# Expert value sums of a two-layer decoder in four 64x64 quadrants of TensorE

## The chip, the cores and the metric

The kernel runs on one core of a Trainium2 chip, as one launch. The metric is its device time in microseconds; a time of the kernel before is the median of three runs. Profiles show one execution of the program.

## The reference

Two decoder layers on 256 tokens of width 1024, all in float32. Each layer has a mixer (gated linear and stick-breaking attention in layer 0, block attention and a linear recurrence in layer 1), a cross-attention into 256 memory tokens, and then an expert network, which is the part that matters here:

```python
def peer_ffn(xn, wq, subkeys, u, v):
    ...
        top_s, pos = lax.top_k(cand, K)                 # 8 heads, K = 16
        eidx = jnp.take_along_axis(cidx, pos, axis=-1)  # 128 experts of 16384 a token
        g = jax.nn.softmax(top_s, axis=-1)
        ue = u[eidx]
        ve = v[eidx]
        act = jax.nn.gelu(jnp.einsum('td,thkd->thk', xi, ue).astype(jnp.float32), approximate=False)
        return jnp.einsum('thk,thkd->td', (g * act).astype(ve.dtype), ve)
```

Every token picks 128 experts. For each it needs the expert's row of `u` (1024 numbers, for a dot product with the token) and its row of `v` (1024 numbers, which is added to the token's output with a weight).

## The kernel before

Activations are kept with features on the 128 partitions and tokens along the free axis; dense weights come through a ring of four 2 MB buffers, loaded from the SP queue. PSUM has eight banks of 512 float32 columns, given out in the order of a written list, `psum_jobs` (L153); `job(name)` in the TensorE program waits until the bank's last user has freed it, and `full`/`copied` (L411, L421) let the other engines wait for a bank's filling and emptying.

The expert network works in **units** (`UNITS = 256` a layer, 512 in all). Unit `u` is the `k`-th expert (of 128) of each of the 128 tokens of token tile `t`, `u = 128 t + k`. Its steps, each on an engine of its own:

- GpSimd (L1700 to L1712) gathers 128 rows of 8 KB, the `u` and the `v` row of each token's expert side by side, into one of eight slots of `arena`. Ahead of it stands `taken` (L455), the wait until the unit that used the slot eight units ago has been summed.
- VectorE (`unit`, L1416) multiplies the `u` half with the tokens and reduces: one number per token. While the first tile's units run, VectorE also does the routing (top-k) of the rest, in layer 0 and layer 1 alike.
- ScalarE (L1000 to L1007) applies the gelu, multiplies with the gate, and writes the 128 gains as a diagonal 128x128 matrix into one of four buffers (`diag`); ahead of the write it waits with `taken` for the unit four back.
- TensorE (L667 to L681) multiplies the diagonal with the slot's `v` half, 512 columns at a time, and adds up over the 128 units of a tile in two PSUM banks, `acc.0` and `acc.1`. The last matmul of a unit raises `expert_mm`, on which `taken` waits.

After 128 units ScalarE copies both banks to `yrow` (tokens on the partitions), TensorE turns `yrow` with eight 128x128 transposes into features on the partitions (`back`, L657), and VectorE adds the result to `xT` (L1423). For the first tile this happens a few units into the second tile; for the second tile it stands at the end of the layer, and in layer 1 at the end of the kernel, ahead of the store.

`mm` (L515) and so L516 is the line of nearly every matmul; a transpose in `back` is L663. L882 is the line of nearly all work on ScalarE. A float32 matmul leaves two records in the trace, each with a weight load of its own; a transpose leaves one.

Of the kernel before, what the change touches and what calls it, by code (L numbers as in the profile page):

```python
# [15 lines left out]
D = 1024  # L16
T = 256
M = 256
P = 128
# [4 lines left out]
BANK = 512  # L24
# [9 lines left out]
PE_H, PE_K, PE_KEYS, PE_DQ = 8, 16, 128, 128  # L34
EXPERTS = PE_KEYS * PE_KEYS
PAIRS = PE_H * PE_K
# [20 lines left out]
LEVELS = [P >> i for i in range(8)]  # L57
CONSTS = {}
for _name, _n in (("ident", P), ("ones", P), ("head_ones", P), ("rot", P), ("tri", P),
                  ("past", 3 * P), ("causal", 3 * P), ("iota", PE_K), ("inv_freq", 1),  # L60
                  ("levels", 8 * P)):
    CONSTS[_name] = (sum(n for _, n in CONSTS.values()), _n)
NCONST = sum(n for _, n in CONSTS.values())
# [3 lines left out]
UNITS = PAIRS * TT  # L67
DIAGS = 4
# [9 lines left out]
def constants():  # L78

    c = np.zeros((P, NCONST), np.float32)  # L80

    def put(name, a):
        at, n = CONSTS[name]
        c[:, at:at + n] = np.asarray(a, np.float32).reshape(P, n)

    p, f = np.arange(P)[:, None], np.arange(P)[None, :]
    put("ident", p == f)
    put("ones", np.ones((P, P)))
    put("head_ones", p // 64 == f // 64)

    rot = np.zeros((P, P))
    for m in range(P):
        half = m % 64 // 32
        rot[m + 32 if half == 0 else m - 32, m] = -1.0 if half == 0 else 1.0
    put("rot", rot)
    put("tri", p >= f)

    put("past", np.concatenate([p < f, np.ones((P, P)), p < f], 1))

    low = np.where(f <= p, 0.0, -1e30)  # L100
    put("causal", np.concatenate([low, np.zeros((P, P)), low], 1))

    lev = [(p // (2 * m) == f // (2 * m)) & (p % (2 * m) < m) & (f % (2 * m) >= m) for m in LEVELS[1:]]
    put("levels", np.concatenate(lev + [p == f], 1))
    put("iota", np.broadcast_to(np.arange(PE_K), (P, PE_K)))
    put("inv_freq", 10000.0 ** (-(np.arange(P) % 32).astype(np.float64) * 2 / MO_D))
    return c
# [105 lines left out]
def trunk(nc, d, out_d):  # L213
# [8 lines left out]
    with ExitStack() as ctx:  # L222
# [3 lines left out]
        def sem(name):  # L226
            return ctx.enter_context(nc.semaphore(name))
# [27 lines left out]
        iota = sb("iota_bf", [P, PE_K], BF)  # L255
        ones_row = cst[:, CONSTS["ones"][0]:CONSTS["ones"][0] + 1].to_broadcast([P, T])

        def const(name):
            at, n = CONSTS[name]
            return cst[:, at:at + n]  # L260
# [5 lines left out]
        ident, ones, head_ones = const("ident"), const("ones"), const("head_ones")  # L266
# [78 lines left out]
        yrow = kv[:, 0:D]  # L345
        dots = red[:, PAIRS:2 * PAIRS]

        diag = const('levels').rearrange('p (n m) -> p n m', m=P)[:, 0:DIAGS, :]
# [54 lines left out]
        gelu_done = sem("gelu_done")  # L403
        gain_done = sem("gain_done")
        weighed = sem("weighed")
        expert_mm = sem("expert_mm")
        stored = sem("stored")

        block = ctx.enter_context(nc.Block())
# [44 lines left out]

        def taken(eng, l, u):  # L455

            eng.wait_ge(expert_mm, l * UNITS + u + 1)


        @block.sync  # L460
# [36 lines left out]
        def _(pe):  # L497
            seen = [0]

            def job(name):  # L500

                n = JOB[name]
                assert n == seen[0], (name, n, seen[0])
                seen[0] += 1
                if n >= BANKS:
                    pe.wait_ge(psum_free[n % BANKS], n // BANKS)
                return psum[:, n % BANKS, :], psum_full[n % BANKS]
# [7 lines left out]
            def mm(out, lhsT, rhs, start=True, stop=True):  # L515
                return nc.tensor.matmul(out, lhsT, rhs, start=start, stop=stop)  # L516
# [117 lines left out]
            def peer(l):  # L634
                b = AT[f"sub{l}"]
                sub = ring[:, b % RING, 0:16 * PE_KEYS].rearrange("p (c n) -> p c n", n=PE_KEYS)
                for g in range(4):
                    w = weights(f"pq{l}{g}")
                    for i in range(2):
                        features(f"pq{l}.{2 * g + i}", w, 2 * P * i, hT, norm=f"ffn{l}" if g == i == 0 else None)  # L640
                    for n in X_ROWS[g]:
                        o, done = job(f"xr{l}.{n}")
                        for c in range(4):
                            last = nc.tensor.transpose(o[:, c * P:(c + 1) * P],
                                                       hT[:, 4 * (n % 2) + c, (n // 2) * P:(n // 2 + 1) * P], ident)
                        last.then_inc(done, 1)
                    copied(pe, f"pq{l}.{2 * g}", f"pq{l}.{2 * g + 1}")
                    if g == 0:
                        pe.wait_ge(w_loaded[b % RING], 16 * (b // RING + 1))
                    for t in range(TT):  # L650
                        o, done = job(f"ps{l}.{4 * t + g}")
                        for c in range(4):
                            last = mm(o[:, c * P:(c + 1) * P], qpT[:, g % 2, c, t * P:(t + 1) * P],
                                      sub[:, 4 * g + c, :])
                        last.then_inc(done, 1)

                def back(t):  # L657

                    copied(pe, f"acc{l}.{t}.0", f"acc{l}.{t}.1")
                    for b in range(2):  # L660
                        o, done = job(f"back{l}.{t}.{b}")
                        for c in range(4):
                            last = nc.tensor.transpose(o[:, c * P:(c + 1) * P],  # L663
                                                       yrow[:, (4 * b + c) * P:(4 * b + c + 1) * P], ident)
                        last.then_inc(done, 1)

                for t in range(TT):  # L667
                    (o0, done0), (o1, done1) = job(f"acc{l}.{t}.0"), job(f"acc{l}.{t}.1")
                    for k in range(PAIRS):
                        u = t * PAIRS + k  # L670
                        pe.wait_ge(weighed, l * UNITS + u + 1)
                        v = slot[slot_of(u)][:, D:2 * D]
                        first = mm(o0, diag[:, u % DIAGS, :], v[:, 0:BANK], k == 0, k == PAIRS - 1)
                        last = mm(o1, diag[:, u % DIAGS, :], v[:, BANK:D], k == 0, k == PAIRS - 1)
                        if k == PAIRS - 1:
                            first.then_inc(done0, 1)
                        last.then_inc(expert_mm, 1)
                        if u == PAIRS + BACK_LAG + 1:
                            back(0)
                    pe.wait_ge(expert_mm, l * UNITS + (t + 1) * PAIRS)  # L680
                    pe.sem_inc(done1, 1)  # L681
                back(1)


# [6 lines left out]
            o, done = job("gg")  # L691
            for k in range(KC):
                last = mm(o[0:GLA_RANK, 0:T], w_gg[:, k, :], hT[:, k, :], k == 0, k == KC - 1)
            last.then_inc(done, 1)
            copied(pe, "gg")
            o, done = job("gate")
            for a in range(2):
                last = mm(o[:, a * T:(a + 1) * T], gate_up[:, a * P:(a + 1) * P], ggT[0:GLA_RANK, :])
# [15 lines left out]
            for li in range(len(LEVELS) + 1):  # L714
# [7 lines left out]
                for par in range(2):  # L722
                    r = slice(64 * par, 64 * par + 64)
# [15 lines left out]
            for i in range(2):  # L739
                o, done = job(f"glao{i}")  # L740
# [1040 lines left out]
```

## Time and profile before

| | |
|---|---|
| median of 3 runs | 1932.71 us (1931.68 to 1933.12) |
| span of the profiled execution | 1928.8 us |
| TensorE matmul busy | 1591.4 us (83%), 4638 records |
| VectorE, ScalarE, GpSimd busy | 52%, 34%, 27% |
| mean granted TensorE clock | 0.984 of 2.4 GHz |
| bytes moved by DMA | 610.20 MB, of which the gathers 536.90 MB |

The span is from the first instruction to the last; the runs' time has some microseconds around it. A matmul's busy time in the records includes the time until its result is out, so records in a row overlap. Layer 0's gather begins near 302 us and its stream ends near 990, layer 1's runs from 1247 to near 1920.

### The profile page before, as it was taken

The numbers are of one execution on the slowest core, as the hardware profiler recorded it, in microseconds if no ns is written. First come the engines' busy times: TensorE is split into PE (matmuls) and PEld (weight loads), VectorE is DVE, ScalarE is ACT, GpSimd is POOL, SyncE is SP. The second block draws the span as 40 slices with busy tenths as digits, with TensorE's granted clock in tenths as the row PEclk, the third lists the DMA queues.
The fourth block names the chain that finished last, engine by engine and source line by source line (L and its number), as shares of the span: only waits on it lengthen the run. The fifth ranks groups of instructions, "written<-read, shape, count | busy, mean of one in ns | idle before, by whom it ended". The sixth has DMA issues, their size and how long they took to land.

```text
span 1928.8 us, 15560 instructions
## 1 busy us (share of the span) xinstructions
PE 1591.4 (83%) x4638; PEld 806.3 (42%) x4638; DVE 1011.3 (52%) x2487; ACT 646.9 (34%) x1897; POOL 514.9 (27%) x516
## 2 busy tenths in 40 slices
PE   7999989767877877787779989997788777877876
PEld 4777778222322222222237666763232222222222
DVE  3432238688544554445441632489874445444454
ACT  1243221423433333333332433123343333333333
POOL 0000001434433433333300000015444343333331
PEclk9999999999999999999989999999999999999999
DMA  8321224999999999999933222359999999999996
GB/s 304 131 88 44 101 108 184 390 416 421 422 421 422 421 422 422 421 421 422 421 154 131 88 104 93 118 221 422 421 421 421 422 421 421 422 421 422 421 421 287
DMA packets 107540, 610.20 MB, mean 316 GB/s; under 512 B 10032, under 2 KB 10176, under 8 KB 41280
## 3 DMA queue, kind: packets, MB, share of 16 engines
q0 software_dynamic: 73728, 536.90, 67.1%
q1 hardware_dynamic: 33728, 72.30, 10.3%
q8 instruction: 37, 0.61, 0.1%
q14 instruction: 47, 0.39, 0.1%
HBM read 608.12 MB, written 1.05 MB: 316 GB/s over the span
## 4 chain that ended last, share of the span: by engine, by line
DMA 45%; PE 38%; DVE 9%; ACT 5%; issue 2%; POOL 0%; SPq 0%; DVEq 0%; PEldq 0%; ACTq 0%
DMA arena<-in_experts,idxT 45%; PE psum L516 37%; DVE arena L1416 5%; ACT cst L882 1%; ACT gains L882 1%; ACT arena L882 1%; ACT gelus L882 1%; ACT L882 1%; DVE red L1385 1%; DVE kv L1377 0%; POOL arena L1710 0%; DMA vecs<-in_vecs 0%; ACT sqb L882 0%; DVE kv L1383 0%; DVE red L1200 0%
## 5 line engine op out<-in xcount | busy, mean ns | idle before, releaser
L516 PE MATMUL psum<-arena,cst 128*128 128x512 f32 (+2 forms) x2112 | 1029.4, 616 | 283.6 <-ACT cst L882 279.1
L1416 DVE CUSTOM_DVE_ANT_0 arena<-arena,xrow 128x1024 f32<-128x1024 f32 x512 | 624.4, 1224 | 537.7 <-DMA arena<-in_experts,idxT 537.0
L1710 POOL DMA_INDIRECT arena<-in_experts,idxT x512 | 514.7, 1005 | 1387.8 <-PE psum L516 790.0
L516 PEld LDWEIGHTS psum<-arena,cst 128*128 128x128 f32 x2112 | 367.1, 191 | 942.5 <-ACT cst L882 645.7
L882 ACT ACTIVATE gelus<-red 128x1 f32<-128x1 f32 x512 | 103.6, 202 | 770.2 <-DVE red L1416 769.9
L516 PE MATMUL psum<-hT,ring 128*128 128x256 f32 x1280 | 293.3, 390 | 6.1 <-DVE hT L1215 6.1
L516 PEld LDWEIGHTS psum<-hT,ring 128*128 128x128 f32 x1280 | 248.9, 196 | 47.5 <-issue 9.8
L882 ACT ACTIVATE cst<-cst,gains 128x128 f32<-128x128 f32 x512 | 206.2, 403 | 23.2 <-PE psum L516 6.7
L882 ACT ACTIVATE gains<-gelus,gateT 128x1 f32<-128x1 f32 x512 | 150.8, 294 | 17.0 <-ACT gelus L882 0.2
L882 ACT ACTIVATE arena<-psum 128x512 f32<-128x512 f32 (+3 forms) x89 | 47.8, 545 | 304.3 <-PE psum L516 304.0
L516 PE MATMUL psum<-mixT,ring 128*128 128x256 f32 x256 | 57.4, 387 | 2.5 <-DVE mixT L1689 2.5
L516 PE MATMUL psum<-arena 64*128 64x128 f32 (+4 forms) x320 | 52.0, 317 | 4.9 <-DVE arena L1521 2.4
L516 PEld LDWEIGHTS psum<-mixT,ring 128*128 128x128 f32 x256 | 49.7, 195 | 10.8 <-DVE mixT L1689 3.3
L1223 DVE TENSOR_TENSOR xT<-xT,psum 128x512 f32<-128x512 f32 x16 | 11.0, 688 | 72.8 <-PE psum L516 72.8
L516 PE MATMUL psum<-ring,arena 128*128 128x128 f32 (+1 forms) x192 | 44.6, 384 | 2.9 <-issue 2.9
L516 PEld LDWEIGHTS psum<-arena 64*128 64x128 f32 (+2 forms) x320 | 35.7, 177 | 20.0 <-issue 10.5
L1416 DVE DVE_READ_ACCUMULATOR2_ANT red<- 128x1 f32 x512 | 42.5, 83 | 0.0
L516 PE MATMUL psum<-ring,hT 128*128 128x512 f32 x96 | 42.3, 595 | 0.0
L882 ACT ACTIVATE sqb<-xT 128x512 f32<-128x512 f32 x24 | 14.4, 625 | 81.2 <-DVE xT L1223 77.3
L516 PEld LDWEIGHTS psum<-ring,arena 128*128 128x128 f32 x192 | 27.1, 191 | 18.3 <-issue 17.8
L1533 DVE COPY_PREDICATED arena<-cst,psum 128x512 f32<-128x512 int32 x16 | 11.7, 730 | 40.7 <-PE psum L516 40.4
L516 PE MATMUL psum<-arena,ring 128*128 128x256 f32 x128 | 28.1, 380 | 1.6 <-ACT arena L882 1.6
(161 smaller groups left out, 672.1 us busy)
## 6 DMA issues: line engine op xcount, KB each, us to landing
ring<-in_peer_wq SPq DMA_DIRECT2D x8, 2048.0 KB, 8.1
ring<-in_ev_w_in SPq DMA_DIRECT2D x6, 2048.0 KB, 11.8
ring<-in_od_w_in SPq DMA_DIRECT2D x5, 2048.0 KB, 33.0
ring<-in_xa_wkv SPq DMA_DIRECT2D x4, 2048.0 KB, 7.9
arena<-in_experts,idxT POOLq DMA_INDIRECT x512, 15.3
ring<-in_ev_w_out SPq DMA_DIRECT2D x2, 2048.0 KB, 7.8
ring<-in_xa_wq SPq DMA_DIRECT2D x2, 2048.0 KB, 9.2
ring<-in_xa_wo SPq DMA_DIRECT2D x2, 2048.0 KB, 7.7
```

The source lines that it names most:

```text
L516: return nc.tensor.matmul(out, lhsT, rhs, start=start, stop=stop)
L882: return nc.scalar.activation(out, in_, f, **k)
L1223: V.tensor_tensor(x2, x2, pairs(o), ALU.add).then_inc(bank_free(name), 1)
L1385: link(V.tensor_reduce(eidx[:, cols], h_.rearrange("p (n c) j -> p n (c j)", c=2), X, ALU.add))
L1416: V.tensor_tensor_reduce(out=ut, in0=ut, in1=xrow[:, u // PAIRS, :], scale=1.0, scalar=0.0, op0=ALU.mult, op1=ALU.add, accum_out=dots[:, k ...
L1533: ins = V.copy_predicated(attn[:, par].rearrange("p a t q -> p (a t) q"), msk, o.rearrange("p (n q) -> p n q", q=P))
L1710: nc.gpsimd.indirect_dma_start(slot[slot_of(u)], None, d["experts"], bass.IndirectOffsetOnAxis(ap=idxT[:, u:u + 1], axis=0))\
```

## The change

Each unit's value sum was two matmuls with a 128x128 diagonal, one for each half of the 1024 columns. Now it is four, each with a 64x64 diagonal block: rows 0 to 63 and 64 to 127 of the slot separately (the other two blocks of a diagonal matrix are zero). For the first 512 columns the rows go straight: rows 0 to 63 of the slot to partitions 0 to 63 of the bank. For the last 512 columns they go crossed: rows 0 to 63 to partitions 64 to 127. So the four matmuls use the four 64x64 quadrants of the array. `expert_mm` becomes two semaphores, one for each half of the rows, and `taken` waits for both. Both banks of a tile are signalled as done after the last unit has ended on both halves; before, the first bank was signalled by its own last matmul. The crossed bank is put straight in `back`: its four blocks are multiplied with a permutation matrix, `swap`, which is new among the constants, and the other four with the identity; both are float32 matmuls and no longer transposes.

```diff
-                  ("past", 3 * P), ("causal", 3 * P), ("iota", PE_K), ("inv_freq", 1),
+                  ("past", 3 * P), ("causal", 3 * P), ("iota", PE_K), ("inv_freq", 1), ("swap", P),
...
+    put("swap", (p + 64) % P == f)
...
-        expert_mm = sem("expert_mm")
+        expert_mm = [sem(f"expert_mm{r}") for r in range(2)]
...
         def taken(eng, l, u):
 
-            eng.wait_ge(expert_mm, l * UNITS + u + 1)
+            for r in range(2):
+                eng.wait_ge(expert_mm[r], l * UNITS + u + 1)
...
                         for c in range(4):
-                            last = nc.tensor.transpose(o[:, c * P:(c + 1) * P],
-                                                       yrow[:, (4 * b + c) * P:(4 * b + c + 1) * P], ident)
+                            last = mm(o[:, c * P:(c + 1) * P], yrow[:, (4 * b + c) * P:(4 * b + c + 1) * P],
+                                      const("swap") if b else ident)
                         last.then_inc(done, 1)
...
-                    (o0, done0), (o1, done1) = job(f"acc{l}.{t}.0"), job(f"acc{l}.{t}.1")
+                    acc = [job(f"acc{l}.{t}.{b}") for b in range(2)]
                     for k in range(PAIRS):
                         u = t * PAIRS + k
                         pe.wait_ge(weighed, l * UNITS + u + 1)
                         v = slot[slot_of(u)][:, D:2 * D]
-                        first = mm(o0, diag[:, u % DIAGS, :], v[:, 0:BANK], k == 0, k == PAIRS - 1)
-                        last = mm(o1, diag[:, u % DIAGS, :], v[:, BANK:D], k == 0, k == PAIRS - 1)
-                        if k == PAIRS - 1:
-                            first.then_inc(done0, 1)
-                        last.then_inc(expert_mm, 1)
+                        for b in range(2):
+                            for r in range(2):
+                                rows_in = slice(64 * r, 64 * r + 64)
+                                col = 64 * (r ^ b)
+                                o, done = acc[b]
+                                last = mm(o[col:col + 64], diag[rows_in, u % DIAGS, rows_in],
+                                          v[rows_in, b * BANK:(b + 1) * BANK], k == 0, k == PAIRS - 1)
+                                if b == 1:
+                                    last.then_inc(expert_mm[r], 1)
                         if u == PAIRS + BACK_LAG + 1:
                             back(0)
-                    pe.wait_ge(expert_mm, l * UNITS + (t + 1) * PAIRS)
-                    pe.sem_inc(done1, 1)
+                    for r in range(2):
+                        pe.wait_ge(expert_mm[r], l * UNITS + (t + 1) * PAIRS)
+                    for o, done in acc:
+                        pe.sem_inc(done, 1)
                 back(1)
```

## Rows read from the trace of the kernel before

**Rows 1.** The page: its head and the engines' busy time, share and instructions.
```profile
span 1928.8 us, 15560 instructions
PE 1591.4 (83%) x4638; PEld 806.3 (42%) x4638; DVE 1011.3 (52%) x2487; ACT 646.9 (34%) x1897; POOL 514.9 (27%) x516
```
**Rows 2.** The page's chain that ended last, shares of the span by engine.
```profile
DMA 45%; PE 38%; DVE 9%; ACT 5%; issue 2%; POOL 0%; SPq 0%; DVEq 0%; PEldq 0%; ACTq 0%
```
**Rows 3.** Stretches: busy us and count by engine, clock, DMA share, GB/s.
```profile
600.00:700.00 100.00, 80.34 (x171) 28.18 (x170) 50.94 (x83) 36.97 (x122) 38.60 (x41) 1.00 1.01 422
360.00:370.00 10.00, 6.87 (x15) 2.12 (x13) 6.28 (x22) 2.70 (x9) 3.30 (x4) 1.00 1.02 414
400.00:430.00 30.00, 18.55 (x37) 6.58 (x37) 24.98 (x103) 9.00 (x30) 10.63 (x9) 0.97 1.02 417
970.00:980.00 10.00, 7.93 (x16) 2.71 (x16) 4.94 (x8) 3.63 (x13) 1.73 (x2) 1.00 1.02 424
```
**Rows 4.** Timeline, 601 to 605 us: start, duration, instruction [idle before, releaser].
```profile
601.81 1.98 PE L516 MATMUL psum<-arena,cst 128*128 128x512 f32 x4 [0.50 <-ACT cst L882]
...
604.30 1.98 PE L516 MATMUL psum<-arena,cst 128*128 128x512 f32 x4 [0.50 <-ACT cst L882]
```
**Rows 5.** The gathers' line L1710: from issue to landing.
```profile
DMA to landing us min/median/max: 5.3/15.3/22.7
```
**Rows 6.** Timeline of TensorE: 64-row matmuls in two halves, and 128-row ones.
```profile
51.82 0.72 PE L516 MATMUL psum<-arena 64*128 64x128 f32 x8 [2.36 <-DVE arena L1521]
...
61.26 1.71 PE L516 MATMUL psum<-arena 64*128 64x128 f32 x16
...
125.67 3.81 PE L516 MATMUL psum<-arena 128*128 128x128 f32 x32 [1.15 <-DVEq L1548]
```
**Rows 7.** Chain at the start, and the issue of the first constants load.
```profile
1.66 6.21 DMA vecs<-in_vecs
...
cst<-in_consts SPq DMA_DIRECT2D x1, 712.5 KB, 6.2
```
**Rows 8.** The page's DMA queues that carry instructions: packets, MB, share.
```profile
q8 instruction: 37, 0.61, 0.1%
q14 instruction: 47, 0.39, 0.1%
```
**Rows 9.** Start of layer 1's stream: timeline of GpSimd and TensorE, then stretches.
```profile
1284.19 1.43 POOL L1710 DMA_INDIRECT arena<-in_experts,idxT  x1 [28.14 <-PE psum L516]
1289.92 0.93 POOL L1710 DMA_INDIRECT arena<-in_experts,idxT  x1 [4.30 <-PE psum L516]
1292.73 0.94 POOL L1710 DMA_INDIRECT arena<-in_experts,idxT  x1 [1.88 <-PE psum L516]
...
1287.09 22.54 PE L516 MATMUL psum<-arena,cst 128*128 128x512 f32 x48 [3.17 <-ACT cst L882]
...
1290.00:1292.00 2.00, 2.00 (x4) 0.79 (x3) 1.93 (x7) 0.75 (x3) 0.85 (x1) 0.57 0.29 57
1292.00:1294.00 2.00, 2.00 (x6) 0.82 (x5) 1.97 (x15) 0.79 (x3) 0.94 (x1) 1.00 0.90 356
```
**Rows 10.** Timeline of the tail of layer 0, from the last unit's matmuls.
```profile
989.90 1.98 PE L516 MATMUL psum<-arena,cst 128*128 128x512 f32 x4 [0.50 <-ACT cst L882]
...
991.12 0.60 ACT L882 ACTIVATE kv<-psum 128x512 f32<-128x512 f32 x1 [1.27 <-PE psum L516]
992.01 0.60 ACT L882 ACTIVATE kv<-psum 128x512 f32<-128x512 f32 x1 [0.29 <-PEq L681]
...
992.71 1.06 PE L663 MATMUL psum<-cst,kv 128*128 128x128 f32 x8 [0.82 <-ACT kv L882]
993.37 1.29 DVE L1423 TENSOR_TENSOR xT<-xT,psum 128x512 f32<-128x512 f32 x2 [4.55 <-PE psum L663]
```
**Rows 11.** Timeline: the same pair of matmul records at either level of the clock.
```profile
998.98 1.22 PE L516 MATMUL psum<-red,cst 128*128 128x256 f32 x2 [5.21 <-DVE red L1200]
...
87.40 0.59 PE L516 MATMUL psum<-red,cst 128*128 128x256 f32 x2
```

## The prediction

> **What bounds the kernel now.** I read the page's shares first, then the chain that ended last, then the stretches, then single units. TensorE is the busiest engine by time, 83% [rows 1], and that is the trap of this profile: the chain that ended last runs through DMA for 45% and through TensorE for 38% [rows 2]. The stretches say which of the two it is in the gather. From 600 to 700 us TensorE is busy 80.34 us of 100 while the DMA engines stand at a share of 1.01 and move 422 GB/s [rows 3]; near the stream's end it is 424 GB/s. One unit is one gather of 128 rows of 8 KB, 1.049 MB, so 422 GB/s is one unit each 2.485 us. The timeline shows just that pace: TensorE starts a unit at 601.81 and the next at 604.30, and its four matmul records take 1.98 us, after which it idles 0.50 [rows 4]. A gather lands 15.3 us (median) after its issue [rows 5], which is six units of 2.485 us: the requests wait in a queue. A slot that comes free earlier only makes that queue longer. So a faster value sum is worth nothing in the steady stream, and is worth something only where DMA is not full or the stream has ended: the first units of layer 1, and the tail behind each layer's last unit. The other side of it: TensorE costs nothing more as long as a unit keeps it under 2.485 us.
>
> **What a unit costs after the change.** Before: 2 matmuls of 512 columns, 4 records (an fp32 matmul leaves two), (1.98 - 0.26) / 4 = 0.43 us each and 0.26 for the last to drain [rows 4]. (The same 0.26 is left over in the 32 records of 128 columns that take 3.81 us: 0.11 each [rows 6].) After: 4 matmuls of 64 x 64, 8 records, of 0.43 us each since the 512 columns stay. What counts is how many run side by side. The trace of before has 64-row matmuls, the upper half of the rows and then the lower: 8 of them took 0.72 us, where 8 in line would take 8 x 0.11 + 0.26 = 1.14; 16 took 1.71, in line 2.02 [rows 6]. So two row halves do overlap, well when few are queued on each. Nothing in the trace runs two column halves of the same rows side by side. Bounds for a unit, in recorded time: all four together 2 x 0.43 + 0.26 = 1.12 us; row halves together and column halves staggered by one record 3 x 0.43 + 0.26 = 1.55; column halves in line 4 x 0.43 + 0.26 = 1.98 (as now); nothing together 8 x 0.43 + 0.26 = 3.70. I take 1.55, since the rows show overlap of different parts of the array with fp32 and since two records of one quadrant must follow each other.
>
> **The sum, part by part**, against the profiled span of 1928.8 us; the median of the runs is 1932.71, 3.9 us more, and I add that at the end.
> - *Constant table.* `swap` adds 128 columns, 64 KB, to the first constants load. The first chain item is the DMA of `vecs` just behind it, 6.21 us, on a 712.5 KB load of 6.2 us [rows 7]: 64/712.5 of the 6.2 us would be 0.5, if that load alone set the time; at 422 GB/s it is 0.16. I take +0.2.
> - *Steady stream.* 0, covered by the DMA queue [rows 3, 4, 5]. The second `wait_ge` in `taken` stands before each diagonal on ScalarE and before each gather on GpSimd. GpSimd's issue takes 0.94 us of 2.485 [rows 9] and its wait is for the slot anyway; behind it on its queue are only later gathers. ScalarE's wait is for a unit four back. Both row halves of a unit end together within a record. 0.
> - *More instructions.* 8 more records a unit (4 matmul, 4 weight load) are 4096. The two instruction queues moved 0.61 + 0.39 MB for 15560 instructions [rows 1, 8], 64 bytes each, so 0.26 MB more, on engines that are full: +0.6 us. If they are fetched elsewhere it is 0.
> - *First units of layer 1.* There DMA is starved: GpSimd issues at 1284.19, then only at 1289.92 and 1292.73, released by TensorE's 48 records that begin at 1287.09; DMA moves 57 GB/s from 1290 to 1292 and 356 in the next 2 us, with the clock at 0.57 in the first of these [rows 9]. With units of 1.55 us (twice as long while the clock is low) I put the second and third issue at about 1288.7 and 1290.3, 1.2 and 2.4 us earlier; every later unit of the layer moves with DMA. Bounds: 0 (units as slow as now) to -3.5 (units of 1.12, and the slow filling up to full rate shortened as well). I take -2.4. In layer 0 this doesn't pay, since weight loads fill DMA there: at 360 to 370 us it moves 414 GB/s at 1.02 with TensorE busy 6.87 of 10 [rows 3].
> - *Tail of each layer, twice.* Now: last unit starts at 989.90; the copy of the first half begins at 991.12, as soon as the first matmul is done, the second at 992.01; transposes 992.71, 8 records in 1.06 us; the two additions from 993.37, 1.29 us for both [rows 10]. After: both signals come only after the whole unit. With 1.55 us the copies begin near 991.6 and 992.2, +0.2 for the second. The transposes become fp32 matmuls, 16 records x 0.11 + 0.26 = 2.02 us instead of 1.06; the second addition can't begin before they end, so the pair ends 0.8 us later. Together +1.0 a layer at full clock. At the lower clock a pair of 256-column records takes 1.22 us instead of 0.59 [rows 11]; then the unit ends about 1.6 us later than now and the 16 records cost some 2.7 more, +4.3. Which clock? In the ramps TensorE is busy 6.87 of 10 us and holds 1.00, and from 400 to 430 it is busy 18.55 of 30 and is granted 0.97 [rows 3]; 1.55 of 2.485 is 62%, the same share. I take +1.8 a layer, nearer the full clock: +3.6.
>
> Sum: 0.2 + 0.6 - 2.4 + 3.6 = +2.0. Span 1930.8, time **1934.7 us**. The transposes of the first token tile lie inside the stream and are covered by the 15.3 us queue.
>
> **The rule against this change.** The trace shows 64-row halves overlapping, but each half wrote a bank of its own there [rows 6]. The Trainium skill, "PSUM — Partial Sum Buffer", section "PSUM bank collisions raise a hardware error", says that different row tiles must not access one PSUM bank at the same time. In this change both row halves write one bank, in different partition halves. By that rule, kept by waiting, the time would be that of rival 3. No run here shows it.
>
> **Rivals.**
> 1. *Column halves in line*: the change doesn't do what it says beyond the row halves. Units stay 1.98 us. For it: no row shows column halves together. No gain in layer 1; the tail pays 0.6 for the later first signal and 0.8 for the matmuls: 0.8 + 0 + 2.8 = +3.6, 1936.3.
> 2. *The clock stays at the lower level through the streams.* TensorE streams for less of each unit than now, and the lower level came after stretches in which it did little: 0.57 from 1290 to 1292, after idling 3.17 us before 1287.09 [rows 9]. Units (pitch at most 1.72 us, one unit overlapping the next) still fit under 2.485, but both tails run low: 0.8 - 1.5 + 8.6 = +7.9, 1940.6.
> 3. *One bank at a time.* Both row halves write the same bank, which no row shows, and wait for each other there. Of the four matmuls only the second and third (other rows, other bank) overlap, and the fourth with the next unit's first: three steps of 0.86 and 0.26, 2.84 us for a unit, but a pitch of 1.72, so DMA still sets the stream. Tail: second copy 1.5 later, matmuls 0.8: 0.8 + 4.6 = +5.4, 1938.1.
> 4. *TensorE becomes the bound, clearly slower.* From a pitch of 2.485 us on, each 0.1 us costs 51 us over 512 units. Nothing overlapping is 3.44 us of streaming: 512 x 0.95 = +490, about 2420. The same happens with rival 1 at the lower clock. Against it: the overlapping row halves.
> 5. *All four together at full clock*: 0.8 - 3.5 + 2 x 0.55 = -1.6, 1931.1, no measurable change.
> 6. *Faster*: the longer queue moves DMA from 422 to the 424 GB/s of one stretch [rows 3]: 0.5% of 1272 us is -6, 1928. Against it: share 1.01 already.
>
> **How the numbers follow.** Forecast 0.40 (own range 1932 to 1938), rivals in order 0.20, 0.16, 0.06, 0.07, 0.07, 0.04. About 0.2%, 3.9 us, is what a measurement here tells from no change, so "same" is 1928.8 to 1936.6. Same: 0.36 of the forecast, 0.14 of rival 1, 0.03 of 2, 0.02 of 3, all 0.07 of 5, 0.62. Slower: 0.04 + 0.06 + 0.13 + 0.04 + 0.07 = 0.34. Faster 0.04. The range 1930.5 to 1941.5 leaves out rivals 4 and 6 and the ends of the others.
>
> **What would show each step.** In the stretches of the gather: 422 GB/s and share 1.01 unchanged, units still 2.485 us apart, median landing time longer by what the unit became shorter. A unit's 8 records in about 1.55 us; 1.98 is rival 1, 2.84 rival 3. Granted clock in the stream: near 1 or well below tells the forecast from rival 2. In layer 1 the second gather issued before 1289.9 less whatever the start moved. In the tail, 16 records instead of 8 ahead of the additions and both copies behind one signal. The prediction is wrong if a unit's pitch passes 2.485 us, or if DMA's rate in the stream moves at all.

## The result, and the profile after

The kernel after takes 1933.62 us (median of 20 runs, 1931.27 to 1937.56); the kernel before, run beside it, 1931.01 (20 runs, 1928.13 to 1933.89). The ratio is 1.0014, 95% interval 1.0008 to 1.0021: slower by 2.7 us, with 1.5 to 4.1 in the interval, and within the 0.2% that the prediction calls no change. The prediction's time was 1934.7 us. Ratios and intervals here are estimates from all the runs of a pair and not quotients of the two medians, which scatter more. The profiled executions have spans of 1928.8 us before and 1932.9 us after.

The page after: head, engines, clock in 40 slices, chain, one instruction queue, the gathers' line.

```profile
span 1932.9 us, 20212 instructions
PE 1454.1 (75%) x6718; PEld 604.0 (31%) x6718; DVE 1011.8 (52%) x2487; ACT 646.7 (33%) x1897; POOL 703.2 (36%) x516
...
PEclk9999999656666676666669999997766667666666
...
q8 instruction: 53, 0.87, 0.2%
...
DMA 39%; PE 35%; DVE 9%; issue 7%; POOL 7%; ACT 4%; POOLq 0%; SPq 0%; ACTq 0%; DVEq 0%; PEldq 0%
...
L1718 POOL DMA_INDIRECT arena<-in_experts,idxT x512 | 703.0, 1373 | 1203.4 <-DVE idxT L1394 579.2
```

TensorE's busy time fell by 137 us against [rows 1], and none of it reached the end. Three things are new. The clock row reads 5 to 7 throughout both gather streams, where the mean before was 0.984. GpSimd is busy 188 us more with the same 516 instructions: one gather's issue takes 1373 ns on average (0.94 us at best, 1.9 for many). And the chain has 7% GpSimd and 7% issue where [rows 2] has none and 2%.

The stretches after: busy us and count of PE, PEld, DVE, ACT, POOL, then clock, DMA share, GB/s.

```profile
500.00:600.00 100.00, 69.67 (x320) 10.87 (x312) 49.92 (x83) 38.88 (x123) 60.49 (x40) 0.64 1.01 421
600.00:700.00 100.00, 70.27 (x340) 13.89 (x344) 50.74 (x83) 36.96 (x122) 60.60 (x41) 0.67 1.01 421
```

The last two numbers are those of [rows 3] within 1 GB/s, the clock is not. The timeline of TensorE after, from 602 us: start, duration, instruction, idle time before.

```profile
602.53 1.99 PE L518 MATMUL psum<-arena,cst 64*64 64x512 f32 x8 [0.51 <-ACT cst L890]
605.02 1.78 PE L518 MATMUL psum<-arena,cst 64*64 64x512 f32 x8 [0.50 <-ACT cst L890]
607.50 1.09 PE L518 MATMUL psum<-arena,cst 64*64 64x512 f32 x8 [0.70 <-ACT cst L890]
```

The starts are 2.48 to 2.49 us apart, as in [rows 4]. A unit's eight records take 1.09 us at the upper level of the clock (2.4 GHz) and 1.99 at the lower (1.2 GHz), which is about what [rows 4] shows for the old unit at the upper level (1.98). All four quadrants do run together, and the stream swings between the two levels.

### Where the time went in the trace

The trace can be cut at events that both kernels have. In the table a stream runs, for layer 0, from the first gather's issue to the start of the last unit's dot product on VectorE, and for layer 1 from the start of the first dot product to that of the last; a tail runs from there to the start of the next layer's norm matmul, or to the end; the middle is from that matmul to layer 1's first gather, code that no kernel here touches, with the time that it spent at the lower clock beside it. All are us of the profiled executions. Two stretches are left out: the start up to the first gather, which takes from 300.95 to 303.11 us in these executions and differs by 0.9 between the two of the kernel before, and the 24.0 us from layer 1's first gather to its first dot product. *Null* and *again* are second copies of before and after, the other names are the experiments below.

| kernel | stream 0 | tail 0 | middle (low clock) | stream 1 | tail 1 | span |
|---|---|---|---|---|---|---|
| before | 685.5 | 11.39 | 248.7 (16.3) | 645.7 | 11.41 | 1928.8 |
| null | 685.4 | 11.39 | 248.5 (16.0) | 644.8 | 11.42 | 1926.6 |
| after | 685.6 | 12.65 | 251.6 (25.4) | 643.2 | 13.31 | 1932.9 |
| again | 685.5 | 12.67 | 251.6 (25.4) | 643.2 | 13.30 | 1932.9 |
| straight | 685.5 | 11.89 | 248.5 (16.0) | 646.3 | 11.90 | 1930.8 |
| back_mm | 685.7 | 12.19 | 251.3 (25.1) | 645.9 | 12.21 | 1932.2 |
| freeswap | 685.1 | 11.86 | 248.7 (16.3) | 644.5 | 12.74 | 1929.3 |
| warm | 685.1 | 11.88 | 251.3 (25.1) | 644.6 | 11.86 | 1930.1 |
| warm_free | 685.2 | 11.86 | 252.3 (30.1) | 644.8 | 11.13 | 1932.4 |
| extra256 | 685.3 | 11.38 | 252.3 (30.1) | 645.5 | 11.40 | 1931.7 |
| extra512 | 696.9 | 18.77 | 251.0 (24.8) | 662.5 | 19.16 | 1974.4 |

Before to after: tails +1.3 and +1.9, stream 1 -2.5 (-1.6 against null), stream 0 nothing, the middle +2.9. The middle is longer where it spent more time at the lower clock, and the edit is not in it.

The timeline of both tails after, from the last unit's matmuls to the second addition: layer 0,

```profile
990.57 1.85 PE L518 MATMUL psum<-arena,cst 64*64 64x512 f32 x8 [0.52 <-ACT cst L890]
...
992.63 1.08 ACT L890 ACTIVATE kv<-psum 128x512 f32<-128x512 f32 x2 [2.12 <-PEq L689]
...
993.82 2.02 PE L518 MATMUL psum<-cst,kv 128*128 128x128 f32 x16 [1.40 <-ACT kv L890]
...
995.88 0.69 DVE L1431 TENSOR_TENSOR xT<-xT,psum 128x512 f32<-128x512 f32 x1 [0.20 <-PE psum L518]
```

and layer 1.

```profile
1921.91 1.09 PE L518 MATMUL psum<-arena,cst 64*64 64x512 f32 x8 [0.83 <-ACT cst L890]
...
1923.20 1.08 ACT L890 ACTIVATE kv<-psum 128x512 f32<-128x512 f32 x2 [1.34 <-PEq L689]
...
1924.38 3.47 PE L518 MATMUL psum<-cst,kv 128*128 128x128 f32 x16 [1.39 <-ACT kv L890]
...
1927.89 0.69 DVE L1431 TENSOR_TENSOR xT<-xT,psum 128x512 f32<-128x512 f32 x1 [0.73 <-PE psum L518]
```

In layer 0 the last unit ran at the lower level (1.85 us) and the turning matmuls at the upper (2.02, the value worked out from [rows 6]); from the unit's start to the end of the additions are 6.00 us, where [rows 10] has 4.76. In layer 1 it is the other way round: a unit of 1.09 us lets turning begin 2.47 us after the unit's start, earlier than the 2.81 of [rows 10], and then the 16 records take 3.47 us. The price of the tail depends on the piece on which the low clock falls.

The start of layer 1's stream after, on GpSimd, and the stretches behind it.

```profile
1288.97 1.42 POOL L1718 DMA_INDIRECT arena<-in_experts,idxT  x1 [28.15 <-PE psum L518]
1294.06 0.94 POOL L1718 DMA_INDIRECT arena<-in_experts,idxT  x1 [3.67 <-PE psum L518]
1295.77 1.08 POOL L1718 DMA_INDIRECT arena<-in_experts,idxT  x1 [0.77 <-PE psum L518]
```

```profile
1294.00:1296.00 2.00, 2.00 (x16) 0.77 (x12) 1.19 (x3) 1.87 (x8) 1.17 (x2) 0.51 0.46 102
1296.00:1298.00 2.00, 2.00 (x24) 0.85 (x20) 1.90 (x14) 1.57 (x6) 1.66 (x2) 1.00 0.80 315
```

After the first issue the second comes 5.09 us later and the third 6.80; in [rows 9] it was 5.73 and 8.54. So 0.6 and 1.7 us are won there, at a low clock (0.51) as before.

### What GpSimd's longer issues are

GpSimd's issues are not longer because slots come free earlier. Four lines of GpSimd's timelines, the first two of after, then one of warm (an experiment below: units of 1.09 us throughout) and one of straight (units of 1.93 us):

```profile
602.85 1.92 POOL L1718 DMA_INDIRECT arena<-in_experts,idxT  x1 [0.57 <-issue]
609.42 0.94 POOL L1718 DMA_INDIRECT arena<-in_experts,idxT  x1 [0.85 <-PE psum L518]
```

```profile
602.99 0.94 POOL L1724 DMA_INDIRECT arena<-in_experts,idxT  x1 [1.55 <-PE psum L518]
```

```profile
602.85 1.97 POOL L1718 DMA_INDIRECT arena<-in_experts,idxT  x1 [0.50 <-issue]
```

I read the traces unit by unit, for units 100 to 249 of layer 0. In after, where the unit that freed the slot ran at the lower level of the clock (1.9 us and more, 92 units) the issue took 1.90 us in the median; where it ran at the upper level (under 1.15 us, 32 units) it took 0.94. So the long issues go with the slots that come free late. What makes an issue long is not shown, and nothing in the stream waits for it: its pace is that of before.

The same reading shows what the second wait in `taken` costs. From the end of the unit eight back to the issue that it releases are 0.27 us in before, null, back_mm and extra256, with one semaphore, and 0.81 to 0.83 in straight, after, again, freeswap, warm and warm_free, with two. No run has the second semaphore by itself, so this may in part be the row halves. The time from a gather's issue to its dot product is 15.34 us before, 15.67 in warm and 14.93 in after: with units 0.89 us shorter throughout, 0.56 goes into the later issue and 0.33 into a longer wait for DMA.

### The profile page after: what moved, and what is told of

It reads as the page before. It is cut to its first block, busy times and chain, and to the rows that moved or that the text cites. A ratio compares the mean times of both kernels' runs of the same rounds, so it can differ in the third digit from the quotient of the medians.

```text
span 1932.9 us, 20212 instructions
## 1 busy us (share of the span) xinstructions
PE 1454.1 (75%) x6718; PEld 604.0 (31%) x6718; DVE 1011.8 (52%) x2487; ACT 646.7 (33%) x1897; POOL 703.2 (36%) x516
## 4 chain that ended last, share of the span: by engine, by line
DMA 39%; PE 35%; DVE 9%; issue 7%; POOL 7%; ACT 4%; POOLq 0%; SPq 0%; ACTq 0%; DVEq 0%; PEldq 0%
DMA arena<-in_experts,idxT 38%; PE psum L518 34%; POOL arena L1718 7%; DVE arena L1424 5%; ACT cst L890 1%; ACT gains L890 1%; ACT arena L890 1%; ACT gelus L890 1%; DVE red L1393 0%; DVE kv L1385 0%; DMA vecs<-in_vecs 0%; ACT sqb L890 0%; DVE rstd L1316 0%; DVE rstd L1304 0%; DVE red L1208 0%
## 5 line engine op out<-in xcount | busy, mean ns | idle before, releaser
L518 PE MATMUL psum<-arena,cst 64*64 64x512 f32 (+1 forms) x4160 | 881.0, 928 | 424.7 <-ACT cst L890 417.6
L1718 POOL DMA_INDIRECT arena<-in_experts,idxT x512 | 703.0, 1373 | 1203.4 <-DVE idxT L1394 579.2
L518 PEld LDWEIGHTS psum<-arena,cst 64*64 64x64 f32 (+1 forms) x4160 | 155.5, 178 | 1144.0 <-ACT cst L890 1099.2
```

Source lines behind the costliest of these rows:

```text
L1718: nc.gpsimd.indirect_dma_start(slot[slot_of(u)], None, d["experts"], bass.IndirectOffsetOnAxis(ap=idxT[:, u:u + 1], axis=0))\
```

## Experiments

Medians are in us; each ratio is against the kernel before, run beside it in one of three groups: warm, freeswap, warm_free and back_mm (median of before there 1930.37, 33 runs), straight, extra256, extra512 and thin_before (1929.55, 23), the others (1931.09, 23).

### How many quadrants run together, and what the crossing brings

*straight* takes the kernel after and sends both column halves of a row half through the same quadrant, so nothing is crossed and `back` keeps its transposes.

```diff
-                                col = 64 * (r ^ b)
+                                col = 64 * r
...
-                            last = mm(o[:, c * P:(c + 1) * P], ..., const("swap") if b else ident)
+                            last = nc.tensor.transpose(o[:, c * P:(c + 1) * P], ..., ident)
```

> The changed kernel with both halves of the columns straight: rows 0 to 63 to partitions 0 to 63 in both banks, so two of the four quadrants are used; turning by transposes. Tells what the crossing does. If quadrants are what runs side by side, a unit takes 1.98 us at full clock instead of 1.09, row halves together and column halves in line. The clock then tells what it follows: near 1 if it follows the time that TensorE is at work, near 0.65 or below if it follows how much of the array is at work; at the lower clock with half the array a unit streams for 3.44 us, over 2.485, and the time goes up by hundreds of us. Otherwise time 1932 to 1934.

Measured: 1933.83 (11 runs), ratio 1.0018 (1.0009 to 1.0026). Timeline of one unit and the stretch from 600 us of straight:

```profile
602.59 1.93 PE L518 MATMUL psum<-arena,cst 64*64 64x512 f32 x8 [0.56 <-ACT cst L890]
```

```profile
600.00:700.00 100.00, 78.72 (x330) 20.09 (x332) 50.75 (x83) 37.01 (x123) 74.49 (x41) 1.00 1.01 421
```

The row halves run together (nothing together would be 3.70 us), the column halves in line. It is the crossing that takes a unit from 1.93 to 1.09 us, and it is also what takes the clock from 1.00 to 0.67: with TensorE busy 78.72 of 100 us the level held, with 70.27 it did not. In both kernels the two row halves write one bank, in different partitions, and neither waited for the other: with waits there a unit of after would be 2.84 us (rival 3) and one of straight 3.70. The Trainium skill, "PSUM — Partial Sum Buffer", "PSUM bank collisions raise a hardware error", quotes both wordings: row tiles not in one bank at a time, and two engines free to use one bank as long as their accesses lie in different quadrants of it. The runs behave as the second, which is said there of two engines. The Trainium skill, "TensorE: Matmul & The Clock Gate", section "Measured speedup vs the span model", says that a pack of tiles takes the time of one matmul plus some nanoseconds a tile; 1.09 us for four against 2 x 0.43 + 0.26 = 1.12 agrees.

### Is the low clock the price?

*warm* adds to the kernel after, ahead of each unit's wait, four matmuls with a block of zeros as weights, in the same four quadrants, so that TensorE is busy more of each unit (all units but the first and the last of a tile).

```diff
+                        for b in range(2 if 0 < k < PAIRS - 1 else 0):
+                            for r in range(2):
+                                rows_in = slice(64 * r, 64 * r + 64)
+                                col = 64 * (r ^ b)
+                                mm(acc[b][0][col:col + 64], const("causal")[rows_in, P:P + 64],
+                                   cst[rows_in, 0:BANK], False, False)
                         pe.wait_ge(weighed, l * UNITS + u + 1)
```

> The changed kernel, and ahead of each unit's wait for its diagonal four more 64x64 matmuls with zeros as weights (they add zero), for all units but the first and last of a tile. They fill TensorE's idle time. Theory (the lower granted clock costs in the tails): the clock in the stream rises from 0.65 to near 1, the last unit and the 16 records of the turning run at full clock, each layer's tail 0.5 to 1.5 us shorter; 1 to 2.5 us less than the changed kernel's 1933.6, so 1931 to 1932.5, ratio to the kernel before 1.000. Rival (the loss is in the extra instructions and the constant): no gain, or 0.6 us more for 4000 more records, 1934.

Measured: 1934.01 (11), ratio 1.0019 (1.0010 to 1.0028). Timeline and stretch of warm:

```profile
601.97 1.04 PE L518 MATMUL psum<-cst 64*64 64x512 f32 x8
603.55 1.09 PE L518 MATMUL psum<-arena,cst 64*64 64x512 f32 x8 [0.54 <-ACT cst L896]
```

```profile
600.00:700.00 100.00, 79.93 (x644) 22.94 (x640) 50.45 (x83) 36.98 (x122) 40.17 (x40) 0.97 1.01 421
```

The clock came back to 0.97 with TensorE busy 79.93, and the tails fell from 1.26 and 1.90 above before to 0.49 and 0.45. So the low clock costs 0.8 and 1.4 us in the tails. The stream did not move by it at all. The median did not follow the tails: 1931 to 1932.5 was expected, and it is 1934.0, no better than after's. "What the clock does outside the streams" has what is known of that.

### What the crossed bank costs at the end

*back_mm* takes the kernel before and only turns with matmuls instead of transposes.

```diff
-                            last = nc.tensor.transpose(o[:, c * P:(c + 1) * P], ..., ident)
+                            last = mm(o[:, c * P:(c + 1) * P], ..., ident)
```

> The kernel before with the turning steps alone changed: float32 matmuls with the identity instead of transposes. By the prediction's step (16 records instead of 8, the pair of additions ends 0.8 us later) +0.8 us in each layer's tail, +1.6 in all, ratio 1.0008. Rival: the additions hide it, 0.

Measured: 1934.44 (11), ratio 1.0019 (1.0010 to 1.0028). Timeline of its tail of layer 0:

```profile
991.73 2.02 PE L516 MATMUL psum<-cst,kv 128*128 128x128 f32 x16 [0.83 <-ACT kv L882]
992.89 0.69 DVE L1423 TENSOR_TENSOR xT<-xT,psum 128x512 f32<-128x512 f32 x1 [5.05 <-PE psum L516]
993.79 0.69 DVE L1423 TENSOR_TENSOR xT<-xT,psum 128x512 f32<-128x512 f32 x1 [0.20 <-PE psum L516]
```

Each tail is 0.80 us longer, the step's own number; the time is up by more, 3.7 us by the ratio, and the rest is not in the tails. With straight (+0.50, +0.49, the later first signal alone) the two parts add up to 1.30; the tail of layer 0 after has 1.26.

*freeswap* takes the kernel after, keeps the transposes, and lets VectorE put the crossed bank straight, by two additions of half the tokens each.

```diff
+                        o = o.rearrange("p (c n) -> p c n", n=P)
+                        if b:
+                            step(V.tensor_tensor(xs[:, :, 0:64], xs[:, :, 0:64], o[:, :, 64:P], ALU.add))
+                            xs, o = xs[:, :, 64:P], o[:, :, 0:64]
+                        V.tensor_tensor(xs, xs, o, ALU.add).then_inc(bank_free(f"back{l}.{t}.{b}"), 1)
```

> The changed kernel with the eight turning steps as transposes again; the crossed bank is put straight by the addition on VectorE, which reads the token halves of the transposed bank in swapped order (two additions of half the width). Theory (the float32 matmuls of the turning cost 1 us at full clock and 1.7 to 2 at the lower one in each tail): 8 records instead of 16, 1 to 1.5 us shorter per tail, together 2 to 3 us less than the changed kernel, 1931. Rival (that time is hidden behind the additions): under 0.5 us, 1933.4.

Measured: 1931.15 (11), ratio 1.0003 (0.9994 to 1.0012). Timeline of its tail of layer 0:

```profile
992.27 1.94 PE L665 MATMUL psum<-cst,kv 128*128 128x128 f32 x8 [1.39 <-ACT kv L890]
...
994.25 0.42 DVE L1433 TENSOR_TENSOR xT<-xT,psum 128x256 f32<-128x256 f32 x1 [0.17 <-PE psum L665]
994.59 0.41 DVE L1435 TENSOR_TENSOR xT<-xT,psum 128x256 f32<-128x256 f32 x1
```

Even with the eight transposes at the lower clock (1.94 us, against 1.06 in [rows 10]) this tail is 0.8 us shorter than after's, and that of layer 1 0.6, where 1 to 1.5 each was expected. Of the versions with four quadrants this one and the next, warm_free, have intervals that take in no change; both keep the transposes.

*warm_free* is both edits in one.

> Both of the edits above together: zero matmuls between the units and transposes with the swap in the addition. If tails are where the change loses and the start of layer 1 where it gains about 1 to 2.5 us, this one is faster than the kernel before by 1 to 3 us: 1928 to 1930, ratio 0.9985 to 0.9995. If the gain at the start of layer 1 is not real, it is equal to the kernel before.

Measured: 1929.95 (11), ratio 0.9993 (0.9984 to 1.0002). The last tail, all of it at the upper clock, is 0.28 us shorter than before's; the tail of layer 0 is 0.47 longer. It is the best version of the four quadrants that was tried, and its gain can't be told from zero.

### Who sets the pace of the stream

*extra256* and *extra512* take the kernel before and add to each unit one matmul with weights of zero, of 256 or 512 columns.

```diff
+                        if 0 < k < PAIRS - 1:
+                            mm(o1[:, 0:256], const("causal")[:, P:2 * P], v[:, BANK:BANK + 256], False, False)
                         last = mm(o1, diag[:, u % DIAGS, :], v[:, BANK:D], k == 0, k == PAIRS - 1)
```

> The kernel before with one more matmul of 256 columns with zero weights in each unit. A unit's streaming goes from 1.72 to 2.15 us, still under the 2.485 us in which DMA delivers a unit. Theory (DMA sets the stream): the stream unchanged; +0.4 us at the start of layer 1, and 4000 fewer... no more than +1.5 us in all, ratio under 1.001. Rival (TensorE's time counts in the chain for 38%): +0.43 us x 512 = +220 us.

Measured: 1932.97 (12), ratio 1.0010 (1.0001 to 1.0018); both streams as before (table).

> The kernel before with one more matmul of 512 columns with zero weights in each unit: streaming 6 x 0.43 = 2.58 us, over 2.485. Theory (TensorE is free up to DMA's pace and sets the stream from there): +0.1 us x 508 units = +48 us, and up to 20 more for what a unit waits between its neighbours; TensorE busy near 100% in the stream, DMA share under 1. Rival (a unit must also wait for its diagonal, so gaps stay): +0.5 us or more x 508, +250.

Measured: 1976.23 (5), ratio 1.0238 (1.0224 to 1.0251). The stretch from 500 us of extra512:

```profile
500.00:600.00 100.00, 100.00 (x234) 44.27 (x233) 49.01 (x82) 37.99 (x120) 41.44 (x39) 1.00 1.00 407
```

TensorE work of 0.43 us more a unit lengthens neither stream, 0.86 more costs about 46 us: the edge lies between a pitch of 2.15 and one of 2.58 us, and the 2.485 us of a gather are in that interval. A unit of 1.98 + 0.86 = 2.84 in recorded time has a pitch of 6 x 0.43 = 2.58, 0.095 over it, or 49 us in 512. In the table the streams hold 28 us of it and the tails 15, since TensorE is by then behind VectorE.

### The gain where DMA does not bind

*half_before* and *half_after* gather rows of 4 KB instead of 8 after the first eight units (each slot's second half keeps what the first gather put there), with the same edit in both kernels.

```diff
+                    w_ = 2 * D if u < SLOTS else D
+                    table = d["experts"] if u < SLOTS else d["experts"].rearrange("e (h n) -> (e h) n", n=D)
-                    nc.gpsimd.indirect_dma_start(slot[slot_of(u)], None, d["experts"],
+                    nc.gpsimd.indirect_dma_start(slot[slot_of(u)][:, 0:w_], None, table,
```

> The kernel before, but from the ninth unit of a layer on each gather brings 4 KB rows instead of 8 KB, into the slot's first half alone; the values that are summed are what lay in the slot's second half, so the output is not the reference's, and the work of all engines but DMA is the same. DMA then needs 1.24 us a unit. Theory (TensorE hides behind DMA, by 0.76 us a unit): TensorE becomes the bound, about 1.72 to 1.8 us a unit, near 100% busy; the first 60 units of a layer are paced by VectorE's routing and stay, some 400 of 512 units shrink by 0.7 us: about 1640. Rival (something else paces units at 2.485): 1932.

Measured: 1596.72 (4), ratio 0.8267 (0.8253 to 0.8281).

> The same cut of the gathers in the changed kernel. Theory (four quadrants halve TensorE's share of a unit and the gain is only covered by DMA in the real kernel): a unit is then paced by VectorE (1.31 us) or DMA (1.24), not by TensorE (0.86 at full clock); against the same cut without the change 400 x 0.4 us = 160 less, about 1480. If the clock falls and stays at its lower level, a unit takes 1.72 us of TensorE again and both kernels are equal. This tells whether the clock eats the gain where TensorE would be the bound.

Measured: 1544.84 (4), ratio 0.8006 (0.7994 to 0.8018). The stretch from 600 us, half_before and then half_after:

```profile
600.00:700.00 100.00, 100.00 (x240) 44.72 (x239) 71.17 (x117) 52.74 (x176) 71.79 (x58) 1.00 0.87 298
```

```profile
600.00:700.00 100.00, 70.28 (x516) 13.76 (x506) 78.92 (x129) 56.83 (x191) 73.54 (x64) 0.98 0.93 335
```

Here TensorE is the bound before the change (busy 100 of 100, 58 units in 100 us by GpSimd's count) and stops being it: 64 units, clock 0.98. The same edit now gives 51.9 us, 3.2%. What limits it then is not shown; DMA's share rose from 0.87 to 0.93 and VectorE's busy time from 71 to 79, so DMA is the nearer to full. I had expected 1640 and 1480. The pace before was the 1.72 us a unit that I had named (58 in 100 us), but 335 us less are some 440 units at 0.76 us each, where I took 400 at 0.7; the pace after was 1.56 us, where I had named 1.31.

*thin_before* was a first try at the same: every other gather on the kernel before fetches 16 rows instead of 128.

```diff
+                    n = 16 if (u + u // SLOTS) % 2 else P
+                    nc.gpsimd.indirect_dma_start(slot[slot_of(u)][0:n], None, d["experts"],
+                                                 bass.IndirectOffsetOnAxis(ap=idxT[0:n, u:u + 1], axis=0))\
```

> The kernel before with every other gather cut to 16 of its 128 rows (the other rows keep what lay there: the values of those rows are wrong, the work of all engines but DMA is the same). DMA needs 1.4 us a unit instead of 2.485. Theory: TensorE becomes the bound, 1.72 us a unit at 83% or more busy; the streams of 600 + 600 us shrink by 0.76 x about 480 units, time near 1570.

Measured: 1736.89 (4), ratio 0.8978 (0.8947 to 0.9009), against 1570 expected. The stretch from 600 us:

```profile
600.00:700.00 100.00, 85.83 (x194) 35.59 (x194) 56.96 (x96) 43.33 (x145) 55.28 (x48) 0.98 0.96 282
```

DMA is still at a share of 0.96, moving 282 GB/s. At 48 units in 100 us that is 2.0 us of DMA a unit instead of 2.5, with 56% of the bytes: by this estimate a gather of 16 rows takes some 1.5 us of DMA time against 2.5 for 128. No engine is full, so the run doesn't say what a bound by TensorE would give; the half pair does.

### What the clock does outside the streams

*null* is the kernel before and *again* the kernel after, both unchanged.

> The kernel before once more, unchanged. Every theory expects a ratio of 1; it tells how far medians of some ten runs lie apart by themselves, and whether the stretch of lower clock near 1090 to 1097 us, which some profiles have and the first one had not, comes and goes without any edit.

Measured: 1929.67 (12 runs) against 1931.09 (23), ratio 1.0000 (0.9991 to 1.0008). Two medians of one kernel differ by 1.4 us.

> The changed kernel once more, unchanged, beside the unchanged kernel before. Expected 2 to 3 us over it, as first measured, with 1 to 2 us of it in the two tails, the start of layer 1 giving 1 us back, and the rest coming or going with the place at which the clock falls near 1000 and 1090 us.

Measured: 1933.06 (11), ratio 1.0013 (1.0004 to 1.0021). Span and all segments repeat those of after within 0.2 us.

The middle has about 248.6, 251.3 or 252.3 us and 16, 25 or 30 us of low clock. It is the same within 0.2 us in both copies of before and in both of after, and differs between programs whose code is equal there. One stretch where they part, before and then after:

```profile
1090.00:1100.00 10.00, 8.70 (x42) 5.97 (x43) 7.15 (x19) 6.89 (x19) 0.00 (x0) 1.00 0.00 0
```

```profile
1090.00:1100.00 10.00, 8.65 (x35) 5.86 (x34) 6.87 (x22) 5.40 (x15) 0.00 (x0) 0.83 0.00 0
```

The same shows over the runs, since each has its mean clock. Among the 33 runs of before in the first group those with a mean clock of 0.981 to 0.983 have spans of 1930 to 1932 us in the mean for each clock value, those of 0.984 to 0.987 of 1928 to 1929: 0.6 us for each 0.001 of clock (correlation -0.67; 0.7 and 0.8 in the two other groups). warm_free's profiled execution (1932.4, clock 0.977) is its slowest; its median span is 1928.1. So a comparison of two profiled executions of this kernel carries up to some 4 us of clock luck in dense code.

The slope holds within a kernel and doesn't carry from one to another. Warm and warm_free have the same median clock, 0.979 against before's 0.984, and 0.6 us for 0.001 would make both 3.0 us slower; warm is 3.6 slower and warm_free 0.4 faster. Nor does it fit back_mm: median clock 0.982, and no such slope within its 11 runs. By their ratios warm and back_mm are 3.7 us over before, straight 3.5 and extra256 1.9, while their tails and streams explain about 0, 1.6, 1.8 and 0. So some 2 us, and more in warm, are not located in four edited kernels, and null, with nothing edited, has a median 1.4 us lower than before's. Why the middle falls into one of three lengths, and whether an edit far from it picks one, stays open; with the clock of after's streams in the mean, its runs can't be split this way.

## Why the prediction was right or wrong

The verdict, a change within 0.2%, came from the right mechanism: DMA covers the value sum. That the time itself was met, 1934.7 against 1933.62, is in part luck. The forecast stood on a median before of 1932.71 (three runs) where twenty gave 1931.01, so its +2.0 is to be held against +2.7, and the parts of that +2.0 came out less well than their sum.

- **DMA sets the stream: right.** Stream 0 is 685.1 to 685.7 us in each kernel up to the edge of 2.485 us, at 421 or 422 GB/s and a share of 1.01, whether a unit takes 1.09, 1.93, 1.98 us or, as in extra256, more. Extra512 and the half pair show the bound from both sides. The sign that I named for the cover, a landing time longer by what the unit became shorter, was not seen in that size: in warm, with units 0.89 us shorter, a gather waits 0.33 us longer, and in after 0.41 us less.
- **The second wait in `taken`, 0: wrong in size, harmless in the stream.** Kernels with it issue a gather 0.55 us later after the slot came free. The stream covers that. The start of layer 1 does not: in straight, with units as long as before, the third issue comes 9.03 us after the first (1285.12 to 1294.15) where [rows 9], null and back_mm have 8.54.
- **A unit of 1.55 us: wrong.** It is 1.09, rival 5's 1.12. [rows 6] has small matmuls in two row halves that overlap in part, and I carried "in part" over to 512 columns. The number that mattered was the one record's streaming time plus the drain.
- **The clock stays near full: wrong in the streams, half right where it counts.** I argued that TensorE kept 0.97 at 62% busy and 1.00 at 69% in the ramps; at 70% the stream had 0.67. The premise of rival 2 came true. But the level swings, and the tails met it for one piece each: +1.26 and +1.90 against my 1.8 each and rival 2's 4.3. The sum of the two, 3.2 against 3.6, was close because a unit that was too long stood in for a clock that was too high. Its parts by themselves held: 0.8 for the matmuls (back_mm 0.80), 0.5 for the later signal (straight; I had 0.6).
- **The start of layer 1, -2.4: the right sign, the size in doubt.** Stream 1 is 643.2 in both executions against a mean of 645.5 in before, null and back_mm, -2.2. But null alone is 0.9 below before, and the other three with four quadrants have 644.5 to 644.8, about -0.8. The second and third issues came 0.6 and 1.7 us earlier relative to the first, where I had 1.2 and 2.4; the second wait's 0.55 is about what is missing. Straight, with units of 1.93, gains nothing, as rival 1 had it.
- **Constants, +0.2: in line with the traces.** The first TensorE matmul starts at 11.37 to 11.69 us in the seven executions with `swap` (mean 11.57) and at 11.24 to 11.47 in the seven without (mean 11.32). The ranges overlap, so the size is as forecast only in the mean.
- **More instructions, +0.6: no sign.** The queue q8 grew from 0.61 to 0.87 MB, the 0.26 worked out, and in warm to 1.38, and stream 0 was not longer in either (685.6, 685.1).
- **Missed: the middle.** I gave unchanged code no term, and it holds 2.9 of the 4.1 us between the two profiled executions. Tails, stream 1 and constants sum to 3.2 - 2.2 + 0.2 = +1.2; the other 1.5 of the medians' +2.7 could be half of the middle's, and no run settles it.

## What to carry to other kernels

Ask what binds in the stretch, not which engine is busiest: here the same edit halved TensorE's time for a unit and gave 3.2% where TensorE was full and nothing where DMA was. Work taken from a covered engine is not free either, if the engine then does so little that its clock falls and the next dense piece starts at the lower level. Below some 4 us, cut the trace at shared events and run the kernel before twice, since code that nobody touched moved by 3.8 us here.

## What was not expected of the hardware

- Four 64x64 float32 matmuls of 512 columns, in four quadrants, take as long as one (1.09 us; 1.93 for the four in two quadrants), with two of them writing one bank in different partitions.
- The clock: 0.64 to 0.67 at 70% busy in a regular stream, 1.00 at 79% in straight and 0.97 at 80% in warm, but 0.98 in half_after at 70% with units closer together; the share alone doesn't tell the level.
- GpSimd takes 0.94 us or about 1.9 to issue the same gather. In straight nine issues in ten took the longer time (units 100 to 249), in warm and before hardly any, at one and the same pace of units.
- A gather of 16 rows instead of 128 in every other unit left DMA at a share of 0.96 while its rate fell from 422 to 282 GB/s, so its time goes by more than its bytes; rows of 4 KB reach 335 GB/s at 0.93.
